# Two heads' values side by side, and the router's logits in four column tiles with the gather ahead of the gates

## The chip, the cores and the metric

The kernel runs on one core of a Trainium2 chip. The metric is the device time of one execution in microseconds (us); the time before is the median of three runs. All profile numbers come from one profiled execution of the same program.

## The reference

Two layers over 256 latent tokens of width 1024, with 256 context tokens. Layer 0 runs attention with compressed keys and values (8 heads, 64 value columns each) beside a pooling mixer, then a dense SwiGLU. Layer 1 runs a 2-D Fourier mixing, then a router with the two best of eight experts. What the change touches:

```python
s = einsum('bqhd,bkhd->bhqk', q_nope, k_nope) + einsum('bqhr,bkr->bhqk', q_rope, k_rope)
p = softmax(s * ATTN_SCALE)
attn = einsum('bhqk,bkhd->bqhd', p, v)                 # 8 heads, 512 keys, 256 queries, 64 columns

h = modulate(x, norm_ffn_g[1], sh2, sc2)
logits = h @ router_w                                   # (256, 1024) @ (1024, 8)
top_v, top_i = top_k(logits, 2); top_p = softmax(top_v)
gates = sum(one_hot(top_i) * top_p)
y = sum over e of gates[:, e] * swiglu(h, w1[e], w3[e], w2[e])
```

All is float32. Where speed matters a matrix is split into a high part of shorter mantissa (type fp32r) and the low rest, and three or two products of the parts are added.

## The kernel before, in words

Every engine runs a list of instructions written out by hand, in order; semaphores are the only coupling. TensorE (PE) multiplies and transposes, VectorE (DVE) and ScalarE (ACT) empty its eight banks of 512 columns, SyncE (SP) issues the weight loads in the order of use, each when its buffer is free. A load waits for compute and never for a clock time.

**Attention** (lines 480, 1491 to 1548 and 725 to 740, 1060 to 1090). `ITEMS` are 16 steps, head by head with two blocks of 128 queries. In step n TensorE makes the scores of item n into bank n % 3 (line 1533), turns the normalised probabilities of item n - 2 with four transposes (`turn`, line 1516) and, in every second step from the fourth on, multiplies the values of one head by its turned probabilities (`attend`, line 1526): four matmuls of 128 keys x 64 columns into 64 partitions of bank 5, the lower half for even heads and the upper one for odd. The last two heads follow behind the loop. Between the items stand units of the modulation weights (`ada_unit`, line 1351), matmuls in four column tiles of 32. VectorE takes the maximum (lines 1077, 1078), divides by the sum (1069, 1070), and empties bank 5 into a high and a low part (`attended`, lines 1064 and 877). ScalarE makes the exponentials (734) and copies the turned probabilities (`turn_probs`, 725) into one of two buffers by head. Behind the attention, ScalarE makes the high parts of four pieces of the output projection's weights (639), copies the pool mixer's result (742), VectorE makes its low parts (1090), and TensorE starts the projection (1422).

**Router** (lines 800 to 815, 1135 to 1310, 1651 to 1693). Behind the Fourier projection a mean over the features and a root give the scale of each token. VectorE scales the eight chunks of 128 features (`scale`, line 927), ScalarE adds the shift (`shifts`, line 655), and h is ready chunk by chunk. TensorE first runs four warming matmuls (`keep_warm`, line 1371, a result that nobody reads), then eight matmuls of 128 x 8 router weights, one per chunk, into 8 partitions of bank 4 (line 1656). ScalarE copies the logits (809), TensorE turns them (1660), VectorE runs a chain of small linked instructions on 16 columns (1170 to 1185) to the mask of the two best. Meanwhile TensorE turns h into token rows (1665, sixteen transposes into banks 0 to 3), and ScalarE copies them as the high part `h_tok[0]` (812). After three more warming matmuls TensorE counts ranks and totals (1674 to 1677). VectorE makes from them the table of slots (1189, 1197), then the 0/1 matrix `pick_group` for the first four experts (`group_picks`, line 1238, eight instructions of 96 columns), the low parts `h_tok[1]` (`token_lows`, 1247), the picks of the first expert (1230), the gates and the loop counts (1205 to 1224), and at last its half of the gathered chunks (`take_gathered`, 1254). `gather` (1690) makes for each of eight chunks four matmuls, high and low by two blocks of tokens, into banks 5 to 7; odd chunks are emptied by VectorE, even ones by ScalarE (820), and from the fourth chunk on it waits for them. Then come the experts: matmuls in four column tiles of 32 (1719, 1732), eight experts with three pieces of 96 slots.

Of the kernel before, what the change touches and what calls it, by code (L numbers as in the profile page):

```python
# [73 lines left out]
for _name, _n in (("ident", P), ("mean", P), ("before", P), ("rot", QK), ("iota8", EXPERTS),  # L74
                  ("slot_of", 2 * P), ("edge", NG * 2 * PAD), ("first_slot", MAX_ROUNDS + 1), ("eps", 1)):
    CON[_name] = (_at, _at + _n)
    _at += _n
# [50 lines left out]
def constants():  # L128
# [21 lines left out]
    put("eps", np.full((P, 1), EPS))  # L150

# [30 lines left out]
def build(nc, vec_d, con_d, rope_d, x_d, ctx_d, ada_d, mixa_d, mixb_d, attn_d, mixout_d, ffn_d,  # L182
          dft_d, fnet_d, router_d, moe_d, out_d):
    ctx = ExitStack()
    with ctx:
# [60 lines left out]
        probsT = view(ring, scratch + 10240, 2, 4, T)  # L246
# [25 lines left out]
        logits_e = moe[0:EXPERTS, 0:T]  # L272
# [202 lines left out]

        ITEMS = [(hd, q) for hd in range(HEADS) for q in range(2)]
# [9 lines left out]
        def _(sp):  # L486
# [44 lines left out]
            for n in range(first_unit["mixb"] + 1, len(units)):  # L531
                unit_load(n)

                for h in HALVES_AFTER.get(n, ()):
                    if h >= 2:
                        sp.wait_ge(half_free[h % 2], h // 2)
                    else:
                        sp.wait_ge(pv_ready, HEADS)
                    sp.dma_start(half_view(h), ada_d[1, h // 2][:, (h % 2) * 4 * 512:(h % 2 + 1) * 4 * 512]).then_inc(half_in[h % 2], 16)
# [83 lines left out]
        def _(act):  # L623
# [96 lines left out]
            def turn_probs(n):  # L720
                hd, q = ITEMS[n]
                act.wait_ge(probsT_ready, n + 1)
                if hd >= 2:
                    act.wait_ge(pv_ready, hd - 1)
                nc.scalar.activation(probsT[:, hd % 2, :, q * P:(q + 1) * P],
# [84 lines left out]
            for f in range(4):  # L810
                act.wait_ge(tok_ready, f + 1)
                nc.scalar.activation(h_tok[0][:, f // 2, (f % 2) * 512:(f % 2) * 512 + 512], bank[f][:, :], ACT.Copy).then_inc(tok_taken, 1)
# [54 lines left out]
        def _(dve):  # L867
# [190 lines left out]
            def attended(hd):  # L1058
                dve.wait_ge(pv_ready, hd + 1)
                if hd == 0:  # L1060
                    dve.wait_ge(pooled, NG)
                lo = (hd % 2) * VD
                parts = [p[lo:lo + VD, hd // 2, :] for p in mixed]
                link(nc.vector.tensor_copy(parts[0], bank[5][lo:lo + VD, 0:T]))
                rest(bank[5][lo:lo + VD, 0:T], parts).then_inc(pv_taken, 1)
# [19 lines left out]
            for hd in range(6, HEADS):  # L1085
                attended(hd)
# [83 lines left out]
            link(nc.vector.tensor_copy(logit, bank[4][:, T:T + 16].rearrange("p (a b) -> p a b", a=2)))  # L1170
            for hot, top in ((hot1, top1), (hot2, top2)):
                link(nc.vector.tensor_reduce(top[:, :, 0], logit, AX_X, ALU.max))
                link(nc.vector.tensor_tensor(best, logit, top.to_broadcast(wide), ALU.is_equal))
# [5 lines left out]
                if hot is hot1:  # L1179
                    link(nc.vector.scalar_tensor_tensor(out=logit, in0=hot, scalar=-3e38, in1=logit,  # L1180
# [61 lines left out]
            def token_lows():  # L1242

                for f in (0, 2, 1, 3):
                    dve.wait_ge(tok_taken, f + 1)
                    half = slice((f % 2) * 512, (f % 2) * 512 + 512)
                    nc.vector.tensor_tensor(h_tok[1][:, f // 2, half], bank[f][:, :], plain(h_tok[0][:, f // 2, half]),
                                            ALU.subtract).then_inc(tok_low, 1)
# [59 lines left out]
            token_lows()  # L1308
            picks(0)
            gates()  # L1310
            take_gathered(0)
# [23 lines left out]
        def _(pe):  # L1335
# [184 lines left out]
            def attend(hd):  # L1520
                pe.wait_ge(probsT_taken, 2 * hd + 2)
                if hd >= 1:
                    pe.wait_ge(pv_taken, hd)
                lo = (hd % 2) * VD
                for kt in range(4):
                    last = mm(bank[5][lo:lo + VD, 0:T], values[:, kt, hd * VD:(hd + 1) * VD], probsT[:, hd % 2, kt, :],  # L1526
                              start=(kt == 0), stop=(kt == 3))
                last.then_inc(pv_ready, 1)

            for n, (hd, q) in enumerate(ITEMS):  # L1530
# [6 lines left out]
                if n >= 4 and n % 2 == 0:  # L1537
                    attend((n - 4) // 2)
# [8 lines left out]
            attend(HEADS - 2)  # L1547
            attend(HEADS - 1)
# [10 lines left out]
            pe.wait_ge(pv_taken, HEADS)  # L1559
# [316 lines left out]
```

## Time and profile before

| | before |
|---|---|
| time, median of 3 runs | 1392.29 us (1392.26 to 1392.42) |
| profiled execution | 1392.16 us |
| its span | 1390.4 us |
| mean granted TensorE clock | 0.993 |
| TensorE busy | 1340.2 us (96%) |
| VectorE busy | 418.4 us (30%) |
| ScalarE busy | 243.1 us (17%) |
| bytes moved | 457.62 MB, mean 329 GB/s |

A record is one instruction of the trace. A float32 matmul is two records, a transpose or an fp32r matmul one. In the chain view, the part that waited is followed back to what released it. PE is TensorE's matmuls and PEld its weight loads, which overlap them.

### The profile page before, as it was taken

What the parts mean: (1) busy time and instruction counts of PE and PEld (TensorE: products, weight loads), DVE (VectorE), ACT (ScalarE), POOL (GpSimd) and SP (SyncE); (2) the same over time, 40 slices, a digit from 0 to 9 for tenths busy, and PEclk for the clock granted to TensorE, in tenths of its full rate; (3) what the DMA queues carried; (4) which work ended last, traced back from release to release, by engine and by line L of the source; (5) the groups of instructions that cost most, each with busy time, mean ns of one, the idle gap of its engine ahead of it and who ended that gap; (6) DMA issues with size and microseconds to landing.
All of it is one profiled execution on the core that took longest, in us unless ns stands there. A gap on an engine that the chain in (4) does not pass through costs nothing.

```text
span 1390.4 us, 28609 instructions
## 1 busy us (share of the span) xinstructions
PE 1340.2 (96%) x12750; PEld 703.5 (51%) x12750; DVE 418.4 (30%) x814; ACT 243.1 (17%) x418; POOL 21.7 (2%) x36
## 2 busy tenths in 40 slices
PE   5899899999999999999999999999999999999997
PEld 3755699999989433333333333343333333333333
DVE  2655569888464310011011011012001101101103
ACT  2444453333353200000000000000000000000001
POOL 2210000000000000000000000000000000000000
PEclk9899999999999999999999999999999999999999
DMA  9666159997436396998999899899799999989981
GB/s 384 269 234 255 62 199 350 369 379 299 168 145 240 136 395 271 414 421 338 414 420 400 354 421 420 332 399 416 292 414 421 380 374 420 413 337 421 421 335 36
DMA packets 58772, 457.62 MB, mean 329 GB/s; under 512 B 6656, under 2 KB 6784, under 8 KB 7584
## 3 DMA queue, kind: packets, MB, share of 16 engines
q1 hardware_dynamic: 58656, 455.84, 81.1%
q8 instruction: 102, 1.67, 0.5%
q14 instruction: 14, 0.11, 0.0%
HBM read 454.76 MB, written 1.05 MB: 328 GB/s over the span
## 4 chain that ended last, share of the span: by engine, by line
PE 94%; DVE 3%; DMA 1%; ACT 1%; issue 1%; SPq 0%; DVEq 0%; PEldq 0%; ACTq 0%
PE bank L1719 42%; PE bank L1732 21%; PE bank L1605 9%; PE bank L1595 4%; PE bank L1422 3%; PE bank L1351 2%; PE bank L1459 1%; PE bank L1699 1%; PE bank L1526 1%; PE bank L1392 1%; PE bank L1533 1%; PE bank L1644 1%; PE bank L1380 1%; DMA ring<-in_ada 1%; PE bank L1437 1%
## 5 line engine op out<-in xcount | busy, mean ns | idle before, releaser
L1719 PE MATMUL bank<-ring,work 128*32 128x512 f32 (+1 forms) x6144 | 584.8, 539 | 1.1 <-DVE moe L1283 1.1
L1719 PEld LDWEIGHTS bank<-ring,work 128*32 128x32 f32 x6144 | 199.1, 110 | 373.7 <-issue 340.6
L1732 PE MATMUL bank<-ring,moe 128*32 128x512 f32 x2688 | 294.3, 592 | 0.0
L1283 DVE TENSOR_TENSOR moe<-moe,bank 128x256 f32<-128x256 f32 (+1 forms) x96 | 31.4, 382 | 615.0 <-ACT moe L836 615.0
L1732 PEld LDWEIGHTS bank<-ring,moe 128*32 128x32 f32 x2688 | 87.3, 110 | 193.7 <-issue 191.4
L836 ACT ACTIVATE moe<-bank 128x256 f32<-128x256 f32 (+1 forms) x96 | 27.4, 358 | 709.8 <-PE bank L1719 709.8
L1605 PE MATMUL bank<-split 128*128 128x256 f32 x1056 | 131.3, 284 | 0.7 <-PE bank L1380 0.6
L1605 PEld LDWEIGHTS bank<-split 128*128 128x128 f32 x1056 | 128.0, 192 | 2.1 <-ACT split L763 1.3
L934 DVE TENSOR_TENSOR split<-ring,split 128x2048 fp32r<-128x2048 f32 x33 | 75.6, 2290 | 31.5 <-ACT split L769 24.5
L769 ACT ACTIVATE split<-ring 128x2048 fp32r<-128x2048 f32 x32 | 61.3, 1915 | 114.7 <-PE bank L1605 86.0
L949 DVE SCALAR_TENSOR_TENSOR work<-ring,condp,work 128x512 f32<-128x512 f32 x84 | 63.1, 751 | 3.7 <-DVE split L934 1.1
L1595 PE MATMUL bank<-split 128*128 128x256 f32 x480 | 59.5, 284 | 0.3 <-PE bank L1380 0.3
L1595 PEld LDWEIGHTS bank<-split 128*128 128x128 f32 x480 | 58.2, 192 | 0.4 <-issue 0.4
L1422 PE MATMUL bank<-split 128*128 128x256 f32 x384 | 47.0, 284 | 1.8 <-DVE split L1090 1.8
L1422 PEld LDWEIGHTS bank<-split 128*128 128x128 f32 x384 | 46.3, 192 | 2.2 <-DVE split L1090 2.2
L1269 DVE SCALAR_TENSOR_TENSOR xT<-bank,ada,xT 128x256 f32<-128x256 f32 x64 | 26.3, 473 | 62.1 <-PE bank L1699 62.1
L1459 PE MATMUL bank<-split 128*128 128x256 f32 (+1 forms) x192 | 31.1, 326 | 4.8 <-ACT split L639 4.0
L883 DVE TENSOR_TENSOR split<-ring,split 128x1024 fp32r<-128x1024 f32 (+1 forms) x24 | 28.5, 1206 | 16.4 <-ACT split L639 16.0
L1459 PEld LDWEIGHTS bank<-split 128*128 128x128 f32 x192 | 27.6, 201 | 8.1 <-ACT split L639 4.2
L1287 DVE STREAM_TRANSPOSE moe<-moe 128x256 f32<-128x256 f32 (+1 forms) x96 | 31.7, 380 | 0.0
L1351 PE MATMUL bank<-ring,condp 128*32 128x128 f32 x768 | 25.1, 286 | 5.8 <-DMA ring<-in_ada 5.3
L1230 DVE TENSOR_SCALAR tail<-con,work 128x128 f32<-128x128 f32 x36 | 7.9, 282 | 74.8 <-PE bank L1748 74.8
(203 smaller groups left out, 711.8 us busy)
## 6 DMA issues: line engine op xcount, KB each, us to landing
ring<-in_moe SPq DMA_DIRECT2D x336, 1024.0 KB, 12.5
ring<-in_ffn SPq DMA_DIRECT2D x16, 2048.0 KB, 8.6
ring<-in_ada SPq DMA_DIRECT2D x12, 2048.0 KB, 8.9
ring<-in_ada SPq DMA_DIRECT2D x24, 1024.0 KB, 7.0
ring<-in_mixout SPq DMA_DIRECT2D x2, 2048.0 KB, 8.7
ring<-in_fnet SPq DMA_DIRECT2D x2, 2048.0 KB, 8.1
ring<-in_mixa SPq DMA_DIRECT2D x1, 2048.0 KB, 12.1
ring<-in_mixb SPq DMA_DIRECT2D x1, 1664.0 KB, 14.0
```

Of the source, the lines that this page charges most:

```text
L769: nc.scalar.activation(high_d[:, q % SPLITS_DENSE, :], piece_view(q), ACT.Copy).then_inc(high_ready, 1)
L934: nc.vector.tensor_tensor(low_d[:, q % SPLITS_DENSE, :], piece_view(q), plain(high_d[:, q % SPLITS_DENSE, :]), ALU.subtract).then_inc(low_ ...
L949: ins = nc.vector.scalar_tensor_tensor(out=total, in0=half_view(h)[:, k, :], scalar=weight, in1=total, op0=ALU.mult, op1=ALU.add)
L1283: nc.vector.tensor_tensor(gate_e[:, g, 0:n], gate_e[:, g, 0:n], bank[g][:, n:2 * n], ALU.mult).then_inc(e_hidden, 1)
L1287: nc.vector.transpose(hiddenT[phase % 2][:, g, 0:n], gate_e[:, g, 0:n]).then_inc(e_turned, 1)
L1351: last = mm(bank[RUNS[run][2]][32 * j:32 * j + 32, u * P:(u + 1) * P], cond[:, k, :], w[:, k, j * P:(j + 1) * P], start=(k == 0), stop=(k ...
L1422: last = mm(bank[banks[c // 2]][:, (c % 2) * T:(c % 2) * T + T], parts[left][:, k, j * P:(j + 1) * P], source[right][:, k0 + k, :], start= ...
L1459: last = mm(out, parts[left][:, k, lo:hi], h_in[right][:, k0 + k, 0:n], start=((left, right) == PRODUCTS[0] and k0 + k == 0 and opens), st ...
L1595: last = mm(bank[FFN_BANKS[k // 2]][:, (k % 2) * T:(k % 2) * T + T], w[:, j, k * P:(k + 1) * P], hidden_parts[g % 2][:, right, j, :], star ...
L1605: last = mm(bank[kind == "w3"][:, j * T:(j + 1) * T], w[:, k, j * P:(j + 1) * P], h_parts[:, right, k, :], start=(n == 0 and j == 0 and k ...
L1719: last = mm(bank[g][c * QUAD:(c + 1) * QUAD, 0:count * P], x_group[:, 4 * half + k, j * CAP + g * QUAD:j * CAP + (g + 1) * QUAD], source[: ...
L1732: last = mm(bank[3 + n][c * QUAD:(c + 1) * QUAD, :], hiddenT[phase % 2][:, g, blk * QUAD:(blk + 1) * QUAD], source[:, j, n * 512:(n + 1) * ...
```

## The change

- `attend` takes a pair of heads: eight matmuls, the two heads alternating between the lower and the upper 64 partitions of bank 5, in every fourth step from the sixth on. `attended` empties 128 partitions once a pair. The turned probabilities have four buffers by head, two of them in `tail`.
- The router's logits: chunks 0 to 3 and then 4 to 7 are multiplied in four column tiles, each into 8 of 32 partitions. The sum over the four tiles comes with the turning, as a matmul by a 0/1 matrix `fold` where a transpose stood. Half of the transposes of h stand between the first four chunks, the rest behind the second set. The four warming matmuls ahead are gone; those behind the turning are six for three.
- VectorE reads the fresh logits in bank 4 without a copy. `group_picks` is two instructions of 384 columns for eight of 96.
- VectorE's `take_gathered(0)` stands ahead of `picks(0)` and `gates()`. TensorE waits for each high part of the tokens inside the gather, and no longer for all four ahead.

```diff
-        probsT = view(ring, scratch + 10240, 2, 4, T)
+        probsT = [view(t, at + n * 4 * T, 4, T) for t, at in ((ring, scratch + 10240), (tail, 768)) for n in range(2)]
-        logits_e = moe[0:EXPERTS, 0:T]
+        logits_e = moe[:, 0:T]
+        TOK_ORDER, TOK_BANKS = (0, 2, 1, 3), (1, 3, 2, 0)
-                if hd >= 2:
-                    act.wait_ge(pv_ready, hd - 1)
+                if hd >= 4:
+                    act.wait_ge(pv_ready, (hd - 4) // 2 + 1)
+            def take_tok(n):
+                f = TOK_ORDER[n]
+                act.wait_ge(tok_ready, n + 1)
+                nc.scalar.activation(h_tok[0][:, f // 2, (f % 2) * 512:(f % 2) * 512 + 512], bank[TOK_BANKS[f]][:, :], ACT.Copy).then_inc(tok_taken, 1)
-            nc.scalar.activation(logits_e, bank[4][0:EXPERTS, 0:T], ACT.Copy).then_inc(logits_taken, 1)
+            nc.scalar.activation(logits_e, bank[4][:, 0:T], ACT.Copy).then_inc(logits_taken, 1)
+            for n in range(4):
+                take_tok(n)
-                if n >= 5 and n % 2:
-                    attended((n - 5) // 2)
+                if n >= 7 and n % 4 == 3:
+                    attended((n - 7) // 4)
-            link(nc.vector.tensor_copy(logit, bank[4][:, T:T + 16].rearrange("p (a b) -> p a b", a=2)))
+            fresh = bank[4][:, T:T + 16].rearrange("p (a b) -> p a b", a=2)
-                for j in range(GROUP):
-                    for t in range(2):
-                        ins = nc.vector.tensor_scalar(pick_group[:, t, j * CAP:(j + 1) * CAP], C("slot_of")[:, P:P + CAP],
-                                                      rank_at[:, t, bass.ds(GROUP * group + j, 1)], None, ALU.is_equal)
+                spots = [P, GROUP, CAP]
+                for t in range(2):
+                    ins = nc.vector.tensor_tensor(pick_group[:, t, :].rearrange("p (a b) -> p a b", a=GROUP),
+                                                  C("slot_of")[:, P:P + CAP].unsqueeze(1).to_broadcast(spots),
+                                                  rank_at[:, t, bass.ds(GROUP * group, GROUP)].unsqueeze(2).to_broadcast(spots),
+                                                  ALU.is_equal)
-            token_lows()
+            for n in range(4):
+                token_low(n)
+            take_gathered(0)
             picks(0)
             gates()
-            take_gathered(0)
-            def attend(hd):
-                pe.wait_ge(probsT_taken, 2 * hd + 2)
-                if hd >= 1:
-                    pe.wait_ge(pv_taken, hd)
-                lo = (hd % 2) * VD
+            def attend(pair):
+                pe.wait_ge(probsT_taken, 4 * pair + 4)
+                if pair >= 1:
+                    pe.wait_ge(pv_taken, pair)
                 for kt in range(4):
-                    last = mm(bank[5][lo:lo + VD, 0:T], values[:, kt, hd * VD:(hd + 1) * VD], probsT[:, hd % 2, kt, :],
-                              start=(kt == 0), stop=(kt == 3))
+                    for j in range(2):
+                        hd = 2 * pair + j
+                        last = mm(bank[5][j * VD:(j + 1) * VD, 0:T], values[:, kt, hd * VD:(hd + 1) * VD], probsT[hd % 4][:, kt, :],
+                                  start=(kt == 0), stop=(kt == 3), skip_group_check=True)
-                if n >= 4 and n % 2 == 0:
-                    attend((n - 4) // 2)
+                if n >= 6 and n % 4 == 2:
+                    attend((n - 6) // 4)
-            keep_warm(4, 7)
-
-            for k in range(KD):
-                pe.wait_ge(h_ready, KD + k + 1)
-                last = mm(bank[4][0:EXPERTS, 0:T], router[:, k, :], h[:, k, :], start=(k == 0), stop=(k == KD - 1))
+            for half in range(2):
+                for k in range(4 * half, 4 * half + 4):
+                    pe.wait_ge(h_ready, KD + k + 1)
+                    if half == 0:
+                        for t in range(2):
+                            last = nc.tensor.transpose(bank[TOK_BANKS[2 * t]][:, k * P:(k + 1) * P], h[:, k, t * P:(t + 1) * P], C("ident"))
+                            if k == 3:
+                                last.then_inc(tok_ready, 1)
+                for c in range(4):
+                    last = mm(bank[4][c * QUAD:c * QUAD + EXPERTS, 0:T], router[:, 4 * half + c, :], h[:, 4 * half + c, :],
+                              start=(half == 0), stop=(half == 1), skip_group_check=True)
             last.then_inc(logits_ready, 1)
+            for t in range(2):
+                for j in range(4):
+                    last = nc.tensor.transpose(bank[TOK_BANKS[2 * t + 1]][:, j * P:(j + 1) * P], h[:, 4 + j, t * P:(t + 1) * P], C("ident"))
+                last.then_inc(tok_ready, 1)
             pe.wait_ge(logits_taken, 1)
             for t in range(2):
-                last = nc.tensor.transpose(bank[4][:, T + 8 * t:T + 8 * t + 8], logits_e[:, t * P:(t + 1) * P],
-                                           C("ident")[0:EXPERTS, 0:EXPERTS])
+                last = mm(bank[4][:, T + 8 * t:T + 8 * t + 8], logits_e[:, t * P:(t + 1) * P], C("fold"), start=True, stop=True)
-            keep_warm(3, 7)
+            keep_warm(6, 7)
-                        if isinstance(group, int) and n == 1 and k % 4 == 0:
-                            pe.wait_ge(tok_low, k // 2 + 2)
+                        if isinstance(group, int) and k % 4 == 0:
+                            pe.wait_ge(tok_low if n else tok_taken, k // 2 + 2)
             keep_warm(2, 7)
-            pe.wait_ge(tok_taken, 4)
             gather(0)
```

## Rows read from the trace of the kernel before

**Rows 1.** The page: busy time of TensorE, and the chain's shares.
```profile
PE 1340.2 (96%) x12750; PEld 703.5 (51%) x12750; DVE 418.4 (30%) x814; ACT 243.1 (17%) x418; POOL 21.7 (2%) x36
...
PE 94%; DVE 3%; DMA 1%; ACT 1%; issue 1%; SPq 0%; DVEq 0%; PEldq 0%; ACTq 0%
```
**Rows 2.** Windows, the dense stage: us, each engine's busy time, clock, DMA share, GB/s.
```profile
200.00:250.00 50.00, 50.00 (x421) 50.00 (x421) 46.77 (x48) 18.88 (x15) 0.00 (x0) 1.00 0.94 362
```
**Rows 3.** The chain in order of time, attention: start us, us, what.
```profile
134.75 1.94 PE bank L1526 x8
...
140.01 1.94 PE bank L1526 x8
...
151.44 1.89 PE bank L1526 x8
...
154.36 1.91 PE bank L1526 x8
...
160.03 2.06 PE bank L1422 x15
```
**Rows 4.** The chain, the first expert's matmuls in four column tiles.
```profile
471.01 20.78 PE bank L1719 x192
```
**Rows 5.** The timeline of one attention item: start, us, engine, line, what [idle before].
```profile
113.93 1.10 PE L1533 MATMUL bank<-ring 96*128 96x512 f32 x2 [0.18 <-PE bank L1351]
...
114.87 0.60 PE L1516 MATMUL bank<-con,ring 128*128 128x128 f32 x4
...
115.40 1.94 PE L1526 MATMUL bank<-ring 128*64 128x256 f32 x8
...
116.66 0.59 ACT L725 ACTIVATE ring<-bank 128x512 f32<-128x512 f32 x1
```
**Rows 6.** The timeline between the last heads and the output projection.
```profile
151.97 3.88 ACT L639 ACTIVATE split<-ring 128x1024 fp32r<-128x1024 f32 x4
...
158.31 1.67 DVE L1090 SCALAR_TENSOR_TENSOR split<-bank,vec,split 128x256 fp32r<-128x256 f32 x4 [0.91 <-ACT split L742]
```
**Rows 7.** The timeline of the router, from the shifts to the gather.
```profile
449.77 3.30 ACT L655 ACTIVATE ring<-ring,ada 128x256 f32<-128x256 f32 x8 [1.58 <-DVE ring L927]
...
454.48 0.37 ACT L809 ACTIVATE moe<-bank 8x256 f32<-8x256 f32 x1 [1.40 <-PE bank L1656]
...
454.90 0.29 PE L1660 MATMUL bank<-con,moe 8*128 8x8 f32 x2 [0.46 <-ACT moe L809]
...
457.24 1.53 PE L1371 MATMUL bank<-con 128*128 128x256 f32 x6 [0.15 <-PE bank L1665]
...
457.92 0.17 DVE L1184 TENSOR_SCALAR small<-small 128x16 f32<-128x16 f32 x1
...
461.40 0.59 PE L1690 MATMUL bank<-split 128*128 128x384 f32 x2 [0.88 <-DVE split L1238]
...
462.51 4.21 PE L1690 MATMUL bank<-split 128*128 128x384 f32 x14 [0.52 <-DVE split L1247]
```
**Rows 8.** The chain of the router in order of time.
```profile
450.89 3.56 PE bank L1656 x16
...
455.19 1.91 PE bank L1665 x16
...
459.74 1.52 DVE split L1238 x8
461.26 2.39 DVE split L1247 x4
...
467.95 3.07 PE bank L1690 x16
```
**Rows 9.** The chain, the gather of the second group of experts.
```profile
914.23 5.78 PE bank L1690 x32
```
**Rows 10.** Windows, columns as in rows 2: before the output projection, and in the gather.
```profile
158.00:160.00 2.00, 0.19 (x1) 0.00 (x0) 1.69 (x5) 1.04 (x3) 0.00 (x0) 1.00 0.04 8
...
462.00:464.00 2.00, 1.49 (x5) 1.49 (x6) 2.00 (x6) 0.45 (x1) 0.00 (x0) 0.60 0.00 0
```

More of the change, by code:

```diff
@@ L74 @@
 for _name, _n in (("ident", P), ("mean", P), ("before", P), ("rot", QK), ("iota8", EXPERTS),
-                  ("slot_of", 2 * P), ("edge", NG * 2 * PAD), ("first_slot", MAX_ROUNDS + 1), ("eps", 1)):
+                  ("slot_of", 2 * P), ("edge", NG * 2 * PAD), ("first_slot", MAX_ROUNDS + 1), ("eps", 1), ("fold", EXPERTS)):
     CON[_name] = (_at, _at + _n)
@@ L150, in constants @@
     put("eps", np.full((P, 1), EPS))
+    fold = np.zeros((P, EXPERTS))
+    for e in range(EXPERTS):
+        fold[e::QUAD, e] = 1.0
+    put("fold", fold)
     t = np.arange(T)
@@ L1056, in _, with attended @@
             take_rows(1)
-            def attended(hd):
-                dve.wait_ge(pv_ready, hd + 1)
-                if hd == 0:
+            def attended(pair):
+                dve.wait_ge(pv_ready, pair + 1)
+                if pair == 0:
                     dve.wait_ge(pooled, NG)
-                lo = (hd % 2) * VD
-                parts = [p[lo:lo + VD, hd // 2, :] for p in mixed]
-                link(nc.vector.tensor_copy(parts[0], bank[5][lo:lo + VD, 0:T]))
-                rest(bank[5][lo:lo + VD, 0:T], parts).then_inc(pv_taken, 1)
+                parts = [p[:, pair, :] for p in mixed]
+                link(nc.vector.tensor_copy(parts[0], bank[5][:, 0:T]))
+                rest(bank[5][:, 0:T], parts).then_inc(pv_taken, 1)
             def normalised(n):
@@ L1084, in _ @@
             normalised(len(ITEMS) - 1)
-            for hd in range(6, HEADS):
-                attended(hd)
+            attended(HEADS // 2 - 1)
             modulation(2, "ffn_g", 0, 0, 4)
@@ L1169, in _ @@
             wide = [P, 2, EXPERTS]
-            link(nc.vector.tensor_copy(logit, bank[4][:, T:T + 16].rearrange("p (a b) -> p a b", a=2)))
-            for hot, top in ((hot1, top1), (hot2, top2)):
-                link(nc.vector.tensor_reduce(top[:, :, 0], logit, AX_X, ALU.max))
-                link(nc.vector.tensor_tensor(best, logit, top.to_broadcast(wide), ALU.is_equal))
+            fresh = bank[4][:, T:T + 16].rearrange("p (a b) -> p a b", a=2)
+            for hot, top, left in ((hot1, top1, fresh), (hot2, top2, logit)):
+                link(nc.vector.tensor_reduce(top[:, :, 0], left, AX_X, ALU.max))
+                link(nc.vector.tensor_tensor(best, left, top.to_broadcast(wide), ALU.is_equal))
                 link(nc.vector.scalar_tensor_tensor(out=key, in0=best, scalar=-64.0,
@@ L1179, in _ @@
                 if hot is hot1:
-                    link(nc.vector.scalar_tensor_tensor(out=logit, in0=hot, scalar=-3e38, in1=logit,
+                    link(nc.vector.scalar_tensor_tensor(out=logit, in0=hot, scalar=-3e38, in1=fresh,
                                                         op0=ALU.mult, op1=ALU.add))
@@ L1234, in group_picks, with token_low @@
             def group_picks(group):
-                for j in range(GROUP):
-                    for t in range(2):
-                        ins = nc.vector.tensor_scalar(pick_group[:, t, j * CAP:(j + 1) * CAP], C("slot_of")[:, P:P + CAP],
-                                                      rank_at[:, t, bass.ds(GROUP * group + j, 1)], None, ALU.is_equal)
-                ins.then_inc(group_picked, 1)
[L1242 to L1248, printed above, removed]
+                spots = [P, GROUP, CAP]
[4 more added lines that the diff above has]
+                                                  ALU.is_equal)
+                ins.then_inc(group_picked, 1)
+            def token_low(n):
+                f = TOK_ORDER[n]
+                dve.wait_ge(tok_taken, n + 1)
+                half = slice((f % 2) * 512, (f % 2) * 512 + 512)
+                nc.vector.tensor_tensor(h_tok[1][:, f // 2, half], bank[TOK_BANKS[f]][:, :], plain(h_tok[0][:, f // 2, half]),
+                                        ALU.subtract).then_inc(tok_low, 1)
             def take_gathered(group):
@@ L1546, in _ @@
                 turn(n)
-            attend(HEADS - 2)
-            attend(HEADS - 1)
+            attend(HEADS // 2 - 1)
             pe.wait_ge(pooled, NG)
```

15 lines of the change are left out of this document (3 added, 12 removed).

## The prediction

> **What bounds the kernel now.** I read the engine shares and the chain that ended last first [rows 1]: TensorE is busy for 96% of the span and makes 94% of the chain. So the time is a sum of TensorE work and of the few places where TensorE stands still. The window of the dense stage shows TensorE without a gap, with the transfers at 0.94 of their engines' time [rows 2], and the chain of the expert stage is matmuls alone. The diff touches neither stage, so whatever it brings moves their start. It touches two places: attention, from 104 to 160 us, and the stretch from the end of the Fourier projection (447.9 us) to the first expert matmul (471.0 us). For both I read the chain in order of time, then the timeline.
>
> The profiled execution took 1392.16 us, of which 1390.4 are the span and 1.8 lie around it; the median of the runs is 1392.29, 0.13 more. I take differences from the trace and subtract them from the median.
>
> **Part 1, attention.** Before, each head has its own values product: four matmuls, 8 records, 1.87 us till the next one starts, 1.9 in the chain. All eight stand in the chain [rows 3], in the late ones as the last link of a loop: scores, maximum, its scaling, exponential, copy of the turned probabilities, then the product. The loop takes 140.01 - 134.75 = 5.26 us for one head. After, one group of eight matmuls serves two heads, the two alternating between output partitions 0 to 63 and 64 to 127. Nothing in the trace shows two 64-wide tiles. Bounds: if they run one after the other, a pair costs 2 x 1.87 = 3.74 us; if together, 1.87. The nearest row is the expert matmuls in four 32-wide tiles [rows 4]: 192 records of 512 columns in 20.78 us, 0.108 each, while a full-width record of 512 columns takes 0.47 (the scores: 2 records in 114.87 - 113.93 = 0.94 us [rows 5]). Four at once are four times as fast there, each with its own moving operand, as here. I take 1.87 for a pair.
>
> Now the queues, walked through item by item with each instruction's time till the next of its engine, as in rows 5: scores 0.94, transposes 0.53, product 1.87, copy 0.59, and the like for the rest. (The same walk over the order of before ends 0.6 us before the trace; only the difference of two walks is used.) Four product slots of 1.87 go, and with them the 1.05 us in which the last head's product waited for VectorE to empty bank 5 (the seventh starts at 151.44 and lasts 1.89, the eighth starts at 154.36) [rows 3]: 8.5 us in all. What is late in their place: in items without a product, the turning waits for the normalised probabilities, 0.3 us each time, about four times; 0.3 us more at the ada turn. TensorE is then 1.5 us ahead at item 6, 2.7 at item 10 and 4.7 at item 14: in the late part two heads take 8.5 us, not 10.5. The last product waits for the last copied probabilities (0.8 us) and the pool matmuls start 6.8 us earlier than 154.36 + 1.91 = 156.27, at 149.5. There ScalarE becomes the late one: behind its last probabilities copy stand four copies of mixer weights, 3.88 us [rows 6]. They began at 151.97 and now begin 4.7 us earlier, at 147.3, and end at 151.2 to 151.4, while the first pool result is there at 150.6. Before, VectorE's four pool instructions started 158.31 - 156.27 = 2.04 us behind the pool matmuls' start; now 0.94 us behind the first copy's start, at 152.3, take 1.67 and the projection starts at 154.0 and not at 160.03. Sum: 6.0 us earlier. VectorE's product copies are 128 partitions wide and half as many; the instructions take as long by their 256 columns, and four pairs of 0.43 us go, all beside TensorE. The weights are no obstacle: the mixer's weights and the first dense pieces are issued by slots that TensorE frees earlier as well. The wait on the copies of the probabilities (four buffers for two) looks back two pairs and holds nothing up. SyncE's wait for the last product comes before its first half unit and is met long before.
>
> **Part 2, router.** The last of eight shifted chunks is ready at 449.77 + 3.30 = 453.07 [rows 7]. Before, TensorE runs sixteen records one after the other, 3.56 us, ending at 454.45 [rows 8]. After, the first four chunks are done while the others are made, with eight of the sixteen transposes (0.12 us each, 1.91 for sixteen [rows 8]) between them; behind 453.07 stand one set of four column tiles, 0.45 us by the ratio of rows 4, and the pipeline's end: logits ready at 453.65. The copy is 128 partitions of 256 columns, 0.37 as before: 454.07. In between TensorE turns the other eight blocks till 454.5, and the two fold matmuls follow. Two transposes took 0.29 [rows 7]; two full fp32 matmuls are four records, 0.5 to 0.6: 455.05. The first chain instruction then starts at 455.1 (before at 455.23, 0.04 behind the end of the two transposes), and the copy ahead of it is gone, 0.21. The mask is ready 0.34 us earlier, at 457.75 (458.09 before: 457.92 + 0.17). Before, three warming matmuls ran from 457.24 to 458.77 [rows 7], so the ranking matmuls came late; the six of now start at 455.05 and end, at 0.43 each, at 457.65. So the rank arrives at 458.25; before, it came 0.59 us ahead of the picks' start, at 459.15: 0.9 us. The group's picks were 8 instructions in 1.52 us [rows 8]. Now they are 2 of 384 columns; four of 512 took 2.39, 0.60 each, so 0.49 each, 0.98 in all: 0.5 us. They end at 459.8. The first high matmuls follow, and the low ones wait for two subtractions, 1.2 us: 461.05.
>
> Then comes the largest term. Before, the gather stopped at the fifth chunk until VectorE had done the remaining subtractions, the picks and the gates and at last copied the second chunk: 467.95 [rows 8]. After, the copies come directly behind the subtractions. They take 0.49 on ScalarE and 0.55 on VectorE per chunk, against 0.75 us of matmuls per chunk on TensorE, so TensorE is the bound: 30 matmuls at 0.18 to 0.19 (32 records in 5.78 in the later group [rows 9], 16 in 3.07 in rows 8), 5.5 us, ending at 466.6. The expert matmuls start at 466.6, not at 470.95: 4.35 us for the whole part. Cover: picks and gates (3.8 us on VectorE) now lie behind the gather and end at 471; VectorE's first expert work waits for the 20.78 us of matmuls of rows 4. If that cover were gone they would cost the same 3.8. The first weights are there: the transfers' share was 0.00 at 462 to 464 [rows 10], those issued before had landed, and the scratch is released 2.7 us earlier.
>
> **The clock.** The granted clock was 0.60 of full in the window of 462 to 464 (full is 2.4 GHz, the lower level 1.2) [rows 10], and full before 462 and from 466 on. Before it fell TensorE had had short matmuls and pauses of 0.9 and 0.5 us. Before, this cost nothing: 14 gather matmuls took 4.21 us, 0.30 each [rows 7], and VectorE was later still. Now the gather is the bound, and the same slow stretch costs it 14 x 0.11 = 1.6 us. The change also makes new thin places: TensorE has only transposes and small sets from 449.1 to 453.1 where four warming matmuls stood, and pauses of 2.5 to 3 us ahead of the projection, where before they were 1.8 and the clock held [rows 10]. A slow stretch there costs at most 1.7 us in the projection, and 0.5 to 1.2 in the router chain (the sets, the fold and the warming matmuls, at half pace). From nothing to 4.9 us in all; I take 0.8 for part 1 and 1.5 for part 2, since the gather's stretch fell in the trace and the others only might.
>
> Sum: 6.0 - 0.8 = 5.2 and 4.35 - 1.5 = 2.85, together 8.05: 1392.29 - 8.05 = 1384.2.
>
> One rule speaks against the change. The Trainium skill (TensorEngine Tiling (Array Packing), Key Properties) says that tiles of one mode work independently, but a change of the mode drains the array. The trace shows a switch as a small pause: the scores behind an ada unit start 0.18 us after its end [rows 5]. By that the change's new switches, four in the router, cost some 0.3 us and leave the sum as it is; only if passing from one half to the other counted as a switch would the rule turn the sign (third rival).
>
> **Rivals.** (1) The clock holds everywhere: 1392.29 - 10.35 = 1381.9. For it: the clock held at 158 to 160 with 0.19 us of work in two. Against: 462 to 466. (2) The two 64-wide halves run one after the other: a pair takes 3.74, the walk ends 0.7 us behind the old one (the last product then serves both heads behind the last probabilities), and only the router gains: 1390 with slow stretches, 1388.6 without. Against: rows 4. (3) The slower side: each change of half waits for the array to drain. A matmul then costs 0.47 + 0.16, eight of them 5.0; the projection starts 5.9 us later than now, the router gives back 4.35: 1393.9. It decides from 4.8 us for a pair on, where the sum is nil. For it: the pause after a tiled unit [rows 5]; against: 192 tiled records without any [rows 4]. (4) The clock falls in the router and stays low until the gather ends: that part gains nothing and the attention keeps 5: 1387.3. (5) The edits gain as said, but the later stages wait for their transfers, at a share of 0.94: 1392. Against: TensorE had no gap there, and they free their own slots.
>
> **Chances.** Forecast 0.50 (its own range 1382.8 to 1386.3), (1) 0.25, (2) 0.08, (3) 0.04, (4) 0.10, (5) 0.03. The range of 1380.9 to 1388.6 takes in the forecast, (1), (4) and a part of (2). A difference of 0.2%, 2.8 us, is what a measurement tells from none: faster than 1389.5 are the forecast, (1), (4) and half of (2) with a rest for error, 0.90; same 0.06, slower 0.04.
>
> **What would show it.** After: four groups of 8 x 2 product records of 1.9 us, the projection's first matmul near 154; the logits' second set short and directly behind the last shift; the gather without a stop, its end 4 us nearer to the projection's end than the 23.1 us of now; expert turns of the same length; a granted clock below 1 in the gather, perhaps at the projection's start. Product groups of 3.7 us, or a gather still waiting for VectorE, would make it wrong.

## The result, and the profile after

| | before | changed |
|---|---|---|
| time, median of 5 runs | 1392.29 us (1391.28 to 1392.52) | 1383.4 us (1381.51 to 1386.05) |
| profiled execution, its span | 1392.16, 1390.4 us | 1383.4, 1381.6 us |
| mean granted TensorE clock | 0.993 | 0.992 |

The ratio is 0.9937 with a 95% interval of 0.9923 to 0.9952: 8.9 us faster, where 8.1 were forecast. The page of the changed kernel, the rows that answer to [rows 1]:

```profile
PE 1331.2 (96%) x12750; PEld 698.5 (51%) x12750; DVE 413.4 (30%) x787; ACT 242.8 (18%) x418; POOL 21.7 (2%) x36
...
PE 93%; DVE 3%; ACT 2%; DMA 1%; issue 1%; SPq 0%; DVEq 0%; PEldq 0%; ACTq 0%
```

The chain of the changed kernel in order of time, attention (start us, us, what; L1541 is the product, L1548 the scores, L1435 the projection):

```profile
105.85 1.98 PE bank L1548 x4
...
122.64 1.88 PE bank L1541 x16
...
133.58 1.95 PE bank L1541 x16
...
141.93 1.95 PE bank L1541 x16
...
148.73 3.78 ACT split L645 x4
...
153.33 1.67 DVE split L1100 x4
...
155.05 6.98 PE bank L1435 x56
```

Sixteen records take what eight took in [rows 3], two heads take 141.93 - 133.58 = 8.35 us where they took 10.5, and the chain passes from TensorE to ScalarE's four mixer pieces before the projection. The router's chain, to be held against [rows 8]:

```profile
444.96 3.31 ACT ring L661 x8
448.27 0.14 issue
448.40 0.62 PE bank L1675 x8
449.02 1.03 PE bank L1680 x8
450.05 0.36 PE bank L1684 x4
...
453.80 0.19 DVE small L1199
...
454.38 1.03 DVE split L1248 x2
455.41 1.21 DVE split L1259 x2
456.62 0.04 issue
456.66 5.47 PE bank L1708 x30
462.13 12.99 PE bank L1737 x117
```

The gather runs its last 30 matmuls without a stop and the first expert follows at once. (They are fp32r, so here one record is one matmul.) To compare executions I cut the span at four instructions that every version has: first scores, first projection matmul, first shift of the router (`shifts`), first expert matmul (462.07 in the changed kernel's timeline, 470.95 before).

| us | start to scores | to projection | to first shift | to expert | to end |
|---|---|---|---|---|---|
| before | 104.06 | 55.97 | 289.74 | 21.18 | 919.4 |
| changed | 105.85 | 49.20 | 289.91 | 17.11 | 919.5 |
| attn_only | 105.06 | 49.19 | 289.74 | 21.14 | 919.4 |
| router_only | 104.27 | 55.97 | 289.88 | 17.10 | 919.5 |
| pair_serial | 103.37 | 52.44 | 289.86 | 17.11 | 919.5 |
| gather_late | 104.96 | 50.08 | 289.87 | 21.40 | 919.5 |
| after_again | 104.93 | 49.19 | 289.92 | 17.10 | 919.5 |
| warm_gaps | 105.84 | 49.19 | 289.92 | 17.11 | 919.5 |
| cold_gather | 104.01 | 49.20 | 289.89 | 19.38 | 919.5 |
| two_edits | 104.56 | 48.64 | 289.90 | 16.52 | 919.5 |
| logits_plain | 103.63 | 49.20 | 289.90 | 17.09 | 919.5 |
| best | 104.14 | 47.90 | 289.86 | 17.02 | 919.5 |
| best_warm | 102.68 | 47.89 | 289.87 | 16.52 | 919.5 |

pair_by_two, with one execution, lies within 0.15 us of the changed kernel in each column behind the first (49.34 in the second).

So of the 8.8 us between the two spans attention gave 6.77 and the router 4.07, the stretch before the first scores took back 1.79, and 0.2 went elsewhere. The diff does not touch that first stretch. From the two chains of it, first before, then changed (L1365 and L1378 are the same four transposes):

```profile
2.11 7.49 DMA ring<-in_ctx
...
11.67 8.88 PE bank L1437 x16
...
22.58 9.37 DMA ring<-in_ada
...
36.70 0.67 PE bank L1365 x4
```

```profile
2.11 8.11 DMA ring<-in_ctx
...
12.29 9.92 PE bank L1450 x16
...
24.25 9.02 DMA ring<-in_ada
...
38.02 1.13 PE bank L1378 x4
```

The windows of it, again first before, then changed (columns as in rows 2):

```profile
28.00:36.00 8.00, 3.64 (x64) 2.96 (x64) 4.62 (x7) 0.00 (x0) 5.16 (x6) 0.57 1.00 425
36.00:42.00 6.00, 1.29 (x7) 1.06 (x8) 4.56 (x13) 3.71 (x7) 0.00 (x0) 0.76 0.99 410
42.00:50.00 8.00, 8.00 (x54) 8.00 (x54) 7.72 (x15) 8.00 (x15) 0.00 (x0) 0.75 0.69 276
```

```profile
28.00:36.00 8.00, 3.04 (x67) 2.57 (x60) 6.24 (x8) 0.00 (x0) 6.83 (x8) 0.73 0.99 425
36.00:42.00 6.00, 2.07 (x24) 1.18 (x16) 2.91 (x10) 1.93 (x4) 0.00 (x0) 0.50 0.99 419
42.00:50.00 8.00, 6.86 (x37) 6.86 (x38) 7.72 (x14) 8.00 (x15) 0.00 (x0) 0.58 0.91 359
...
444.00:452.00 8.00, 6.03 (x48) 4.08 (x47) 4.55 (x16) 6.20 (x14) 0.00 (x0) 1.00 0.96 378
452.00:463.00 11.00, 10.06 (x62) 7.97 (x64) 7.31 (x21) 3.91 (x7) 0.00 (x0) 1.00 0.29 108
```

The first transfer landed 0.6 us later, the first 16 matmul records took 1.04 us more, and the weights of the fourth modulation unit landed 1.3 us later (33.27 for 31.95). The granted clock accounts for the last 0.46 us: four transposes took 1.13 us at a clock of 0.50, where they had taken 0.67 at 1.00. From 28 to 50 us the clock was low for longer in the changed kernel's execution (a mean of 0.61 for 0.69), but most of that cost nothing: behind the transposes the chain runs through VectorE up to the 112 records at 54.14 and 55.92 us, and the distance of the two executions stays at 1.78 us. In the 16 records the granted clock reads 1.00 in both traces, though the longest of them lasted 1.19 us and the median one 0.59; why they are slow is not shown. In the router and the gather the clock was full, the contrary of what I had priced.

### The profile page after: what moved, and what is told of

Same layout as the page of the kernel before. It is cut to its first block, busy times and chain, and to the rows that moved or that the text cites. A ratio compares the mean times of both kernels' runs of the same rounds, so it can differ in the third digit from the quotient of the medians.

```text
span 1381.6 us, 28571 instructions
## 1 busy us (share of the span) xinstructions
PE 1331.2 (96%) x12750; PEld 698.5 (51%) x12750; DVE 413.4 (30%) x787; ACT 242.8 (18%) x418; POOL 21.7 (2%) x36
## 4 chain that ended last, share of the span: by engine, by line
PE 93%; DVE 3%; ACT 2%; DMA 1%; issue 1%; SPq 0%; DVEq 0%; PEldq 0%; ACTq 0%
PE bank L1737 42%; PE bank L1750 21%; PE bank L1619 9%; PE bank L1609 4%; PE bank L1435 3%; PE bank L1364 2%; PE bank L1472 1%; PE bank L1717 1%; PE bank L1405 1%; PE bank L1658 1%; PE bank L1708 1%; PE bank L1548 1%; PE bank L1450 1%; PE bank L1393 1%; DMA ring<-in_ada 1%
## 5 line engine op out<-in xcount | busy, mean ns | idle before, releaser
L1435 PE MATMUL bank<-split 128*128 128x256 f32 x384 | 47.0, 284 | 2.4 <-DVE split L1100 2.4
L1435 PEld LDWEIGHTS bank<-split 128*128 128x128 f32 x384 | 46.3, 192 | 2.8 <-DVE split L1100 2.8
```

The lines of the kernel that those rows point to most:

```text
L1435: last = mm(bank[banks[c // 2]][:, (c % 2) * T:(c % 2) * T + T], parts[left][:, k, j * P:(j + 1) * P], source[right][:, k0 + k, :], start= ...
```

## The experiments

**attn_only and router_only.** Each half of the diff alone, on the kernel before. The edits are those of the diff.

> The kernel before with the pairs of heads alone. Theory (two 64-wide tiles run together; the edits of the two places add up): a product group of 16 records takes 1.9 us, the time from the first scores to the first matmul of the output projection falls from 55.97 us by 6.8 as in the changed kernel, the router stretch stays at 23.0 us; 1385.5 us. Rival (the gain in attention is only there with the rest of the change): less than 5 us.

1385.74 us (1385.47 to 1386.53, ratio 0.9952, 0.9938 to 0.9965).

> The kernel before with the router's edits alone. Theory: the stretch from the end of the Fourier projection's mean to the first expert matmul falls from 23.0 to 19.0 us, or to 20.5 where the granted clock is low in the gather; 1388.2 to 1389.8 us, and a wider spread of the runs than before. Rival (the spread of the changed kernel comes from its attention part): runs within 0.3 us of each other.

1388.5 us (1387.25 to 1390.03, ratio 0.9972, 0.9961 to 0.9983), beside 1392.62 of the kernel before (1391.11 to 1393.84 in 13 runs). By the table the halves give 6.78 and 4.08 us, what they give together: they add up. I had expected a wider spread with the router's edits. The runs of router_only spread over 2.8 us, but those of the kernel before spread over 2.7 themselves here, so the spread is not shown to be a property of the change.

**pair_serial and pair_by_two.** Only the order of the eight products differs.

```diff
-                for kt in range(4):
-                    for j in range(2):
-                        hd = 2 * pair + j
+                for j in range(2):                                        # pair_serial
+                    hd = 2 * pair + j
+                    for kt in range(4):
...
+                for two, j in ((0, 0), (0, 1), (2, 0), (2, 1)):           # pair_by_two
+                    hd = 2 * pair + j
+                    for kt in (two, two + 1):
```

> The changed kernel with the eight products of a pair issued head by head (four for the lower 64 partitions, then four for the upper ones) and not alternating; same instructions, same waits. Theory (two halves overlap only if neighbours in the queue are of different halves): a group takes 3.74 us, the walk of the prediction then puts the projection 6.6 us later, 1390 us. Rival (the queue overlaps them whatever their order, or the alternation itself costs): 1.9 us a group and 1383.4 us, or less.

1384.51 us (1383.79 to 1385.29). The chain has a number that neither theory had:

```profile
120.16 2.79 PE bank L1541 x16
...
155.81 9.24 PE bank L1435 x75
```

2.8 us a group, between 1.9 and 3.74. That is less than the two heads one after the other, so their products overlap in part. Attention is 3.25 us longer, for four groups that are 0.91 us longer each: nearly all of a group's length shows in the time.

> The changed kernel with the products of a pair issued two by two: two of the lower half, two of the upper, two, two. Head by head a group took 2.79 us, 12 slots of 0.234 for 16 records: as if the second half started when four records of the first were left. Theory (a half can run ahead of the other by about four records, two matmuls): two by two overlaps fully, 1.9 to 2.1 us a group. Rival (only direct neighbours overlap, and head by head gained in another way): 2.6 us or more.

One execution, 1381.64 us. Its chain:

```profile
120.75 1.93 PE bank L1541 x16
```

Two by two overlaps nearly as fully as one by one (1.93 for 1.88 us). So the neighbours need not be of different halves: two matmuls of a half in a row cost almost nothing, four cost 0.91 us a group, and three were not tried. Both runs fit a lead of four records (two matmuls) by which one half runs ahead of the other; how the chip does it is not shown.

**gather_late.** VectorE's copies back behind the gates.

```diff
-            take_gathered(0)
             picks(0)
             gates()
+            take_gathered(0)
```

> The changed kernel with VectorE's copies of the gathered chunks put back behind the first picks and the gates. Theory (the gather's stop was the largest term): VectorE copies its first chunk 4.6 us later, the gather stops at its fifth chunk and ends 4 us later, 1387.4 us. Rival (the gather would have been slow anyway, by TensorE's clock or by the subtractions): under 2 us later.

1387.43 us (1384.64 to 1390.09), 4.0 above the changed kernel. The stretch is 4.3 us longer. Its chain, first in the attention and then in the gather, and the windows around:

```profile
147.88 3.39 PE bank L1541 x16
...
461.44 0.56 DVE work L1266
...
462.04 4.34 PE bank L1708 x16
```

```profile
144.00:152.00 8.00, 5.91 (x33) 3.51 (x32) 2.69 (x8) 6.24 (x9) 0.00 (x0) 0.79 0.00 0
456.00:466.00 10.00, 6.70 (x30) 6.34 (x30) 6.49 (x26) 1.75 (x4) 0.00 (x0) 0.83 0.00 1
```

The stop is back: the second half of the gather starts behind VectorE's copy. Of the 4.3 us, 1.3 are the clock (16 matmuls in 4.34 us, 3.07 in [rows 8]), 3.0 the order. So the move of VectorE's copies is worth 3 of the router's 4.07 us. This execution also shows the thin place that I had named: at the end of the attention, where TensorE had had pauses, the last product took 3.39 us, and the projection came 0.9 us later.

**after_again.** The changed kernel beside the next three.

> The changed kernel once more, beside the kernels of this call. Theory (the two parts add up, 6.8 and 4.0 us from the first scores on, and what moves from run to run is TensorE's clock, at the start of the kernel above all): the span less the start of the first scores is 1275.7 us again within 1 us unless the granted clock is low behind that point, then 1.3 to 2 more; 1382 us. Rival (one of the gains is lost in some runs by waits, not by the clock): that difference moves while the clock is full.

1382.49 us (1381.74 to 1384.07, ratio 0.9926, 0.9914 to 0.9938). From the first scores to the end 1275.7 us, as in the first trace (1381.6 - 105.85).

**warm_gaps.**

```diff
+            keep_warm(4, 7)            # behind the pool matmuls
...
+            keep_warm(2, 7)            # ahead of the first chunk of h
...
+                if half == 0:
+                    keep_warm(1, 7)    # behind the first set of logits
...
+                        if isinstance(group, int) and k == 0 and n:
+                            keep_warm(1, 7)    # ahead of the first low product
```

> The changed kernel with warming matmuls in the new thin places: four behind the pool matmuls, two ahead of the first chunk of h, one behind the first set of logits, one ahead of the gather's first low product. All stand in time in which TensorE waits. Theory (the new pauses let the clock fall in some runs): median 0.3 to 1 us below the changed kernel of this call and a narrower spread. Rival (the clock holds there anyway, the spread is made ahead of the attention): the same median within 0.3 us and the same spread. If a warming matmul is in the way, up to 0.5 us slower.

1382.4 us (1381.64 to 1383.34): 0.1 us below, no gain, as the rival had it. None of its places came later either. In the trace of after_again, its neighbour, the clock was full from the first scores to the end, so there was nothing to win back behind them.

**cold_gather.**

```diff
-            keep_warm(6, 7)
...
-            keep_warm(2, 7)
```

> The changed kernel without its six and two warming matmuls ahead of the gather. Theory (they hold the clock, and the gather, now bound by TensorE, pays for a slow one): a granted clock of half from some point of the router on, the 30 gather matmuls take 7 us and not 5.5, and the median is 1.3 to 2.5 us above the changed kernel of this call. Rival (the warming is of no use): within 0.4 us of it.

1384.57 us (1383.58 to 1385.98), 2.1 above; its stretch is 2.3 longer. Its timeline and window:

```profile
454.81 7.75 PE L1707 MATMUL bank<-split 128*128 128x384 f32 x30 [0.19 <-DVE split L1259]
```

```profile
452.00:463.00 11.00, 9.56 (x44) 8.41 (x47) 5.85 (x12) 2.57 (x5) 0.00 (x0) 0.69 0.11 43
```

Thirty gather matmuls took 7.75 us instead of 5.47 at a granted clock of 0.69. So the warming matmuls that stand there hold the clock, and 2.3 us is what its loss costs: I had said 1.6 from a shorter slow stretch.

**logits_plain.**

```diff
-            for half in range(2): ...                 # two sets in four column tiles, transposes between, fold
+            keep_warm(4, 7)
+            for k in range(KD):
+                pe.wait_ge(h_ready, KD + k + 1)
+                last = mm(bank[4][0:EXPERTS, 0:T], router[:, k, :], h[:, k, :], start=(k == 0), stop=(k == KD - 1))
...
-            keep_warm(6, 7)
+            keep_warm(1, 7)
```

> The changed kernel with the router's logits as before: one matmul after the other into 8 partitions behind four warming matmuls, the transpose in place of the fold, the sixteen transposes of h behind it, and one warming matmul for six. All else as changed. Theory (the traces show the chain's first VectorE instruction 2.16 us behind the last chunk of h before and 2.17 us after, so the four column tiles brought nothing): the stretch from the first shift to the first expert matmul stays within 0.3 us of 17.1. Rival (the prediction: the tiles bring the mask 0.13 us earlier, and the early transposes keep the gather fed): 0.5 us or more longer, the gather's first products waiting for the token rows.

1381.7 us (1381.1 to 1382.54, ratio 0.9921, 0.9906 to 0.9937), not above the changed kernel, and the stretch is 17.09 us for 17.11. Its timeline:

```profile
442.73 3.30 ACT L661 ACTIVATE ring<-ring,ada 128x256 f32<-128x256 f32 x8 [1.58 <-DVE ring L938]
...
448.18 0.17 DVE L1182 TENSOR_REDUCE small<-bank 128x2 f32<-128x16 f32 x1 [2.80 <-PE bank L1673]
```

The chain's first instruction stands 448.18 - 446.03 = 2.15 us behind the last shift, with the tiles 450.43 - 448.26 = 2.17. The column tiles of the change, named in its title, bring nothing as they are built in. The run takes back four things at once: the tiles, the fold, the early transposes and the number of warming matmuls. The changed kernel's timeline shows where the tiles' gain went:

```profile
449.08 0.38 ACT L821 ACTIVATE moe<-bank 128x256 f32<-128x256 f32 x1 [0.82 <-PE bank L1675]
```

ScalarE's copy of the logits starts 0.82 us behind the last shift, where one row of matmuls has it at 447.43 - 446.03 = 1.40. So the tiles bring the logits 0.58 us earlier. The copy ends at 449.46, but TensorE then still makes eight transposes of h (449.02 and 1.03 us in the chain above), and the fold behind them is in the chain from 450.05 on, for 0.36 us where the two plain transposes take 0.29. No run puts those eight transposes behind the fold, so what the tiles are worth without them is not measured.

**two_edits and best.** Versions built from the changed kernel's trace.

```diff
-            mixer_highs("mixout", 0, MIXER_BUFFERS["mixout"])
+            mixer_highs("mixout", 0, 2)          # two_edits; best: 0, 1, and the pool matmuls and
                                                  # VectorE's part of them ahead of the last pair's product
...
+            token_low(0)
             dve.wait_ge(rank_ready, 1)
```

> A better version by the trace of the changed kernel, two moves. ScalarE copies the pool result behind two mixer pieces and not four: the prediction named that queue as the late one, so the output projection should start 0.7 us earlier. VectorE's first subtraction stands ahead of its wait for the rank, in 0.64 us in which it waits anyway: the gather's low products should start 0.6 us earlier. Theory: 1.3 us below the changed kernel of this call. Rival (the projection then waits for its third and fourth piece, the gather for its high parts): under 0.4 us.

1380.78 us (1379.82 to 1383.15, ratio 0.9914, 0.9902 to 0.9927), 1.7 below the changed kernel measured beside it. The traces show 1.15 of it: 0.56 us in the attention and 0.59 in the router.

> The two moves of the run before this one, and the pool matmuls ahead of the last pair's product, with ScalarE copying the pool result behind one mixer piece and VectorE taking it ahead of the last product. In the trace of that run ScalarE waited 1.21 us for the pool matmuls, which stood behind the 1.88 us of the last product. Theory: the first scores to the first projection matmul 47.6 us (48.64 there, 49.20 in the changed kernel), gather and rest as there; 1.0 us below it, 1380.0 us. Rival (the last product's two copies on VectorE now end last): a gain under 0.3 us.

1381.61 us (1378.94 to 1382.27, ratio 0.9915, 0.9900 to 0.9930). The attention is another 0.74 us shorter, but the median is not lower than that of two_edits, which was measured at another time. The trace shows one cause: its router took 17.02 us and not 16.52, and the granted clock was 0.79 in this window ahead of it:

```profile
440.00:448.00 8.00, 6.18 (x43) 3.45 (x43) 3.51 (x10) 5.12 (x13) 0.00 (x0) 0.79 0.85 336
```

**best_warm.**

```diff
             for u in range(4):
+                if u == 3:
+                    keep_warm(10, 5)
                 ada_unit(0, u)
             ada_turn(0)
+            keep_warm(8, 5)
```

> The kernel named best with ten warming matmuls ahead of the fourth modulation unit, where TensorE waits 5.3 us for a transfer, and eight behind the turning of that part, where it waits 4 us. Theory (the 2 us by which executions of one kernel differ come from the slow clock between 28 and 49 us): the fourth unit takes 1.95 us and not 3.64, the first scores start by 102.5 us (103.4 to 105.9 in the traces so far), the median is 1.5 to 2.5 us lower and the spread under 1.5 us. Rival (that stretch is bound by VectorE, ScalarE and transfers): less than 0.5 us. If the warming matmuls themselves run at the lower clock they are in the way: up to 3 us slower.

1379.13 us (1378.28 to 1380.95, ratio 0.9903, 0.9889 to 0.9917), 2.5 below best, measured beside it, and 13.2 below the kernel before: the fastest version. The timeline of its TensorE and the windows:

```profile
27.79 4.55 PE L1385 MATMUL bank<-con 128*128 128x256 f32 x20 [0.17 <-PE bank L1365]
32.27 1.95 PE L1365 MATMUL bank<-ring,condp 128*32 128x128 f32 x64
...
102.68 1.98 PE L1552 MATMUL bank<-ring 96*128 96x512 f32 x4 [0.69 <-ACT ring L717]
```

```profile
28.00:36.00 8.00, 6.94 (x89) 5.85 (x89) 6.25 (x9) 0.00 (x0) 6.13 (x8) 1.00 1.00 423
36.00:42.00 6.00, 5.44 (x33) 4.70 (x32) 5.28 (x14) 5.11 (x10) 0.00 (x0) 1.00 0.98 417
42.00:50.00 8.00, 6.80 (x52) 6.15 (x51) 7.75 (x14) 7.45 (x12) 0.00 (x0) 1.00 0.83 326
```

The clock is full from 28 to 50 us, the fourth modulation unit takes 1.95 us, and the first scores start 0.7 us earlier than in the earliest other trace and 3.2 earlier than in the changed kernel's. The theory asked for 102.5; it was 102.68. Against the trace of best, the first scores start 1.46 us earlier: the unit takes 1.69 us less and starts 0.66 us later, behind the ten warming matmuls, and the four transposes take 0.46 us less. The router gives 0.50 more, where the clock did not fall this time. So the traces show 1.46 us for the warming; the 2.5 between the medians holds that 0.50 and what else varies.

The other half of the theory failed. It wanted a spread under 1.5 us, and it is 2.7. The unit took 3.57 to 3.64 us in all but three of the traces (3.30 and 3.40 in pair_serial and pair_by_two, 1.95 here), so it is a cost of nearly every execution and not what makes them differ. What differs ahead of the first scores is the first transfer (7.38 to 8.31 us) and the first 16 records (8.53 to 10.08 us), and neither is changed here.

## Why the prediction was right, step by step

**The pair (1.87 us).** Right: 1.88, and 1.95 where the group was waited for. The Trainium skill (TensorEngine Tiling (Array Packing), Overview) gives a factor of up to two where a dimension such as the stationary side's columns is 64 or less; the trace agrees, 16 records in 1.88 us for 8 in 1.87. Rivals (2) and (3) are out. The 0.18 us that I had read in rows 5 as the price of a change of tiles is not shown to be one. The same idle time stands between two modulation units of the same tiles, and ahead of the first of them, behind full-width matmuls, there is none (before):

```profile
76.37 1.96 PE L1351 MATMUL bank<-ring,condp 128*32 128x128 f32 x64
78.50 1.95 PE L1351 MATMUL bank<-ring,condp 128*32 128x128 f32 x64 [0.18 <-PE bank L1351]
```

**Attention (6.0 us).** 6.77 measured. The mechanism held, with ScalarE's four mixer pieces as the next late one. Two terms are mis-sized. One is the wait in items without a product: I had two heads at 8.5 us, they take 8.35, and TensorE is 1.6, 3.0 and 5.1 us ahead at items 6, 10 and 14, counted from the first scores, where I had 1.5, 2.7 and 4.7. By it ScalarE's four pieces start 5.0 us earlier, for 4.7. The other is what stands behind: the pieces took 3.78 us, for up to 4.1, and VectorE started 0.83 us behind the first copy (153.33 - 152.50), for 0.94.

**Router, up to the mask (0.34 us earlier).** 0.19 measured: 453.09 - 448.26 = 4.83 us behind the last shift, 5.02 before. The step that failed is "behind 453.07 stand one set of four column tiles, 0.45 us": it and its passage took 0.82 us to the copy, for 0.58, and the eight transposes behind it ended at 450.04, 1.78 us behind the last shift, for 1.43. The fold waits for them, so the chain started no earlier at all, and only the copy that is gone counts. Before, the serial row ended 1.38 us behind the last shift (454.45 - 453.07) and the logits were copied and turned at once: most of it lay beside the shifts, and what the tiles save of the rest goes to the transposes.

**The rank (0.9 us).** 0.54: 453.80 is 5.54 us behind the last shift, 459.15 was 6.08. From the mask (453.09) over the two ranking matmuls to VectorE (453.80) it took 0.71 us, not 0.5.

**The picks (0.54 us).** 0.49: two instructions in 1.03 us.

**The gather (all of the router 4.35 us).** 4.07. The 30 matmuls took 5.41 us to the first expert matmul, for 5.5; what is missing comes from the two steps above. That the order of VectorE's instructions was the largest term is shown by gather_late.

**The clock (2.3 us given away).** Wrong in its place, and about right in its sum by luck. In the profiled execution nothing was lost behind the first scores. Ahead of them, where the diff does nothing, 1.8 us were lost, and the granted clock accounts for 0.46 of these; a transfer and the first 16 records make up the rest. Without allowance the sum is 10.35, and the traces say 10.6 from the first scores on (1286.3 to 1275.7): rival (1)'s mechanism is what the traces of the changed kernel show. The profiled execution, which is also the median one, lies 1.5 us above its 1381.9 because of a stretch that I had left out since no edit touched it. So the forecast of 1384.2 came near by luck: an allowance for one loss was met by another, which the prediction does not name. The clock as such was no phantom: of ten traces that have both parts and the warming ahead of the gather, it fell behind the first scores in two, gather_late (at the attention's end and in the gather) and best (in the router), for 0.9, 1.3 and 0.5 us.

**Transfers (rival 5).** Out: 919.4 and 919.5 us from the first expert matmul to the end.

What stays open: the 0.12 to 0.18 us by which every kernel with the new router is longer from the projection to the first shift; what moves the first transfer and the first 16 records from one execution to the next; and why one unprofiled run of the changed kernel took 1386.05, with a mean clock of 0.988 where the others had 0.991 to 0.993. The clock says that it was slow somewhere for longer; no trace says where.

## What to carry to other kernels

Look for the engine that holds back a consumer by its program order before you shorten matmuls: moving VectorE's copies was worth 3 us, and the tiling of the logits nothing, because most of the serial row already lay beside the shifts and because eight transposes stood in TensorE's order between the faster logits and the fold. When TensorE becomes the bound of a stretch that it used to wait in, its granted clock there turns into time (2.3 us in cold_gather), so count warming matmuls as part of the stretch. Cut two traces at instructions that both have before comparing totals: here a stretch that nobody touched moved by 1.8 us between two executions. And follow the chain through a low clock before you blame it: of those 1.8 us it made 0.46, while in the unit that stands in the chain of every execution filling the waits was worth 1.46.

## What the runs showed of the hardware that was not expected

Products of two 64-wide halves overlap even when they are not neighbours: two by two a group takes 1.93 us, and 1.88 alternating; four and four takes 2.79, where one after the other would be 3.74 (estimate, 2 x 1.87). And the low clock from 28 to 50 us costs 1.69 us in one modulation unit alone (3.64 us before and changed, 1.95 in best_warm at a clock of 1.00).
